# Selection of the samples' keys inside the prompt attention, a step for each head pair, on VectorE

## What is computed

```python
def indexer_select(q_idx, w_idx, k_idx, key_pos, q_pos, n_sel):
    r = jax.nn.relu(jnp.einsum('qhd,sd->qhs', q_idx, k_idx).astype(jnp.float32) * IDX_DIM ** -0.5)
    score = jnp.einsum('qh,qhs->qs', w_idx.astype(jnp.float32), r)
    causal = key_pos[None, :] <= q_pos[:, None]
    _, sel = lax.top_k(jnp.where(causal, score, -jnp.inf), n_sel)
    return sel, key_pos[sel] <= q_pos[:, None]

# a sample: 256 of its 8193 positions; then the rows of keys and values at these positions
        sel, valid = indexer_select(qi, wi, keys_idx, key_pos, q_pos, n_sel)
        k_sel = gather_rows(cache_k, pages, kd, sel, past)
        v_sel = gather_rows(cache_v, pages, vd, sel, past)
```

## Time and profile before

| | us |
|---|---|
| median of 3 runs | 3193.95 (3188.23 to 3194.69) |
| profiled execution | 3187.16 |
| its span, from the first to the last instruction | 3185.3 |
| PE busy in the span | 2648.2 (83%) |
| DVE busy | 1513.6 (48%) |
| ACT busy | 1101.4 (35%) |
| mean granted TensorE clock | 0.921 of full speed |

### The profile page before, as it was taken

How to read it: one execution, slowest core, us unless ns; L and a number is a source line. 1 busy time by engine, 2 the same in 40 slices (tenths; PEclk the granted TensorE clock), 3 DMA queues, 4 the chain that set the end, 5 groups by cost and what they waited for, 6 DMA issues and landing times. The chain is left out here.

```text
span 3185.3 us, 43012 instructions
## 1 busy us (share of the span) xinstructions
PE 2648.2 (83%) x14536; PEld 1497.1 (47%) x14536; DVE 1513.6 (48%) x3685; ACT 1101.4 (35%) x2366; POOL 339.7 (11%) x355
## 2 busy tenths in 40 slices
PE   4798995859988898959878449895989899999978
PEld 1344443538777787845555434343333333333323
DVE  0256454568778786846655755384111111111116
ACT  0223222559876796836444001121111111111111
POOL 0000001010010100011100022043000000100015
PEclk8899997979999999968999779998999999999989
DMA  9312125332171121133100054122999878887867
GB/s 380 137 57 85 47 57 184 126 109 68 37 273 56 67 67 51 34 119 76 31 16 8 8 200 146 69 78 89 392 342 344 342 277 312 321 316 256 303 229 308
DMA packets 242838, 510.69 MB, mean 160 GB/s; under 512 B 23029, under 2 KB 101055, under 8 KB 235248
## 3 DMA queue, kind: packets, MB, share of 16 engines
q1 hardware_dynamic: 195396, 328.71, 29.8%
q0 software_dynamic: 28352, 126.04, 10.8%
q10 hardware_dynamic: 18932, 53.91, 4.3%
HBM read 618.22 MB, written 87.01 MB: 221 GB/s over the span
## 5 line engine op out<-in xcount | busy, mean ns | idle before, releaser
L2740 PE MATMUL routed_ex_pG<-routed_ex_WG,routed_ex_XT 128*64 128x512 f32 x2048 | 485.9, 618 | 69.3 <-issue 29.9
L1838 DVE TENSOR_REDUCE ssqc<-SQ 128x8 f32<-128x512 f32 x516 | 346.2, 683 | 132.9 <-ACT SQ L1644 120.1
L1559 PE MATMUL eK<-WA,LT 128*128 128x272 f32 x1032 | 328.1, 400 | 0.0
L1556 PE MATMUL eK<-dWkv,LT 128*128 128x256 f32 x1032 | 318.3, 391 | 10.9 <-ACT SQ L1644 10.5
L2832 DVE COPY routed_ex_XT<-routed_ex_pX 128x512 f32<-128x512 f32 x128 | 85.6, 689 | 503.6 <-PE routed_ex_pX L2727 503.5
L1644 ACT ACTIVATE SQ<-eK 128x512 f32<-128x512 f32 x516 | 292.5, 603 | 57.0 <-PE eK L1559 41.3
L2740 PEld LDWEIGHTS routed_ex_pG<-routed_ex_WG,routed_ex_XT 128*64 128x64 f32 x2048 | 140.6, 141 | 326.3 <-issue 303.7
L536 PE MATMUL in_pp<-ada_Win,in_hT 128*128 128x512 f32 (+1 forms) x640 | 281.7, 599 | 9.8 <-ACT in_pr L450 9.8
L2760 PE MATMUL routed_ex_pY<-routed_ex_WD,routed_ex_AT 128*64 128x512 f32 x1024 | 232.4, 595 | 1.6 <-DMA routed_ex_WD<-in_w_e_down 1.6
L1559 PEld LDWEIGHTS eK<-WA,LT 128*128 128x128 f32 x1032 | 201.5, 195 | 29.2 <-DVE numc L1837 0.2
L1556 PEld LDWEIGHTS eK<-dWkv,LT 128*128 128x128 f32 x1032 | 191.2, 197 | 46.8 <-ACT SQ L1644 15.6
(11 more groups left out here) (532 smaller groups left out, 3774.2 us busy)
## 6 DMA issues: line engine op xcount, KB each, us to landing
routed_ex_WG<-in_w_e_gu SPq DMA_DIRECT2D x128, 2048.0 KB
routed_ex_WD<-in_w_e_down SPq DMA_DIRECT2D x128, 1024.0 KB
s_yblk<-routed_ex_Y ACTq DMA_DIRECT2D x64, 512.0 KB
ada_Wada<-in_w_ada SPq DMA_DIRECT2D x8, 3072.0 KB, 16.9
s_yblk<-zrows SPq DMA_DIRECT2D x15, 1024.0 KB, 13.7
ada_Win<-in_w_in ACTq DMA_DIRECT2D x4, 2048.0 KB, 18.5
s_tdT<-in_td SPq DMA_DIRECT2D x8, 832.0 KB
s_h<-out_h ACTq DMA_DIRECT2D x9, 512.0 KB, 2.6
```

Source lines behind the costliest of these rows:

```text
L1556: pe.matmul(pK[kn % 3][:, 512 + z:512 + z + HK], key, Wkv[:, 4:8, 0:NOPE], start=True, stop=True)
L1559: pe.matmul(pK[kn % 3][:, z:z + HK + 16], key, WA[:, pr, :], start=True, stop=True).then_inc(s_KN, 1)
L1838: dve.tensor_reduce(ssqc[cg % 2][:, n - 1 - tau, :], SQ[kn % 4].rearrange("p (h d) -> p h d", h=H), AX.X, ALU.add).then_inc(s_red, 1)
L2740: m = pe.matmul(pG[u][r, :], XT[u][:, k, r], WG[2 * u + v][:, k, :], start=(k == 0), stop=(k == KD - 1))
```

## The change

`stage_sample` and `sample_select` are gone. Their work is a list of steps in `attend`, hung on the item number n. On DVE a step is done behind the multiply of pair n-1 (and behind the prompt's own selection step, if there is one), and always before the maxima of pair n+2: `page_rows` at n = 1, `marks` at 2 to 5, `chosen` at 10 to 13, `numbered` at 16 to 19, `digits` at 20 to 22, and `place` at 24 to 55. `place` handles 16 slots (17 at the end of a pair) of one pair of samples: 32 chunks in place of four passes over 129 slots. On PE the products of a chunk stand ahead of the products with the values of the same item, in four column groups (partitions 0, 32, 64, 96 of `pO`); DVE reads their sums ahead of the multiply (`read_sums`) and adds them up in `zparts`. Totals follow at items 8 and 14, a fold over the four groups at item 58, the list's transpose at item 62. The list's transfers are issued by SP between the stores of tiles 6 and 7. `mb` has one buffer now, and POOL waits for the maxima of the tile before.

```diff
-        for st in (stage_ada, stage_in, stage_index, stage_prompt, stage_sample, stage_out, stage_dispatch, stage_routed,
+        for st in (stage_ada, stage_in, stage_index, stage_prompt, stage_out, stage_dispatch, stage_routed,
                    stage_combine):
...
-    mb = [sb(f"mb{i}", [P, H, 2 * P]) for i in range(2)]
+    mb = sb("mb", [P, H, 2 * P])
...
+    CHUNK0, TOTAL01, TOTAL2, FOLD, TURN = 24, 8, 14, 58, 62
+    chunks = [(pr, CH * x, CH * x + CH + (x == 7)) for pr in range(NP2) for x in range(8)]
...
             store(NT - 2)
+            sp.wait_ge(s_zw, 1)
+            for a, n in enumerate(("dpos", "drow")):
+                sp.dma_start(T[n].rearrange("n a b -> a n b"), zlst[:, :, 16 * a:16 * a + 16]).then_inc(s_zo, 16)
+            sp.wait_ge(s_zo, 32)
+            for a, n in enumerate(("dpos", "drow")):
+                sp.dma_start(zld[a], T[n].rearrange("n (s h a) b -> (n s h) (a b)", s=2, h=2)).then_inc(s_zi, 16)
             store(NT - 1)
...
-                if i >= 2:
-                    pool.wait_ge(s_nm, 16 * (i - 1))
+                if i >= 1:
+                    pool.wait_ge(s_nm, 16 * i)
...
                 if n >= 2:
                     pe.wait_ge(s_on, n - 1)
+                if n == TOTAL01:
+                    pe.wait_ge(s_zc, 1)
+                    pe.matmul(pO[0][:, 384:388], c("same_half"), zcnt[:, 0, :], start=True, stop=True)
+                    pe.matmul(pO[0][:, 388:392], c("before_half"), zcnt[:, 1, :], start=True, stop=True)
...
+                elif 0 <= n - CHUNK0 < len(chunks):
+                    k = n - CHUNK0
+                    pr, z, e = chunks[k]
+                    pe.wait_ge(s_zb, k + 1)
+                    for s in range(e - z):
+                        u = s % 4
+                        m = pe.matmul(pO[n % 2][32 * u:32 * u + 32, 256:288], zA[:, s, :],
+                                      zB[:, s, :, :].rearrange("p a b -> p (a b)"), start=(s < 4), stop=(s >= e - z - 4))
+                    m.then_inc(s_zm, 1)
+                elif n == FOLD:
+                    pe.wait_ge(s_zl, 1)
+                    pe.matmul(pO[0][0:32, 384:512], c("fold32"), zparts[:, :, :].rearrange("p n w -> p (n w)"), start=True, stop=True)
+                elif n == TURN:
+                    pe.wait_ge(s_zi, 32)
+                    for a in range(2):
+                        pe.transpose(pO[0][:, 384 + 16 * a:400 + 16 * a], zld[a], c("ident")[0:16, 0:16])
...
+            def place(k):
+                pr, a, b = chunks[k]
+                w = b - a
+                if k:
+                    dve.wait_ge(s_zm, k)
+                link(dve.tensor_tensor(zA[:, 0:w, :], zmark[:, pr, a:b].unsqueeze(2).to_broadcast([P, w, 32]),
+                                       c("iota")[:, 0:32].unsqueeze(1).to_broadcast([P, w, 32]), ALU.is_equal))
+                link(dve.tensor_tensor(zB[:, 0:w, 0, :], zrank[:, pr, a:b].unsqueeze(2).to_broadcast([P, w, 16]),
+                                       c("iota")[:, 0:16].unsqueeze(1).to_broadcast([P, w, 16]), ALU.is_equal))
+                link(dve.tensor_tensor(zB[:, 0:w, 1, :], zB[:, 0:w, 0, :], zrow[:, pr, a:b].unsqueeze(2).to_broadcast([P, w, 16]), ALU.mult))
+                dve.tensor_tensor(zB[:, 0:w, 0, :], zB[:, 0:w, 0, :], zpos[:, a:b].unsqueeze(2).to_broadcast([P, w, 16]), ALU.mult).then_inc(s_zb, 1)
...
             def norm(n):
                 i, g, p = items[n]
                 dve.wait_ge(s_O, n + 1)
+                read_sums(n)
...
                     if g == 1 and FIRST <= i + 1 < NT:
                         select(i + 1 - FIRST, p)
+                    if n == 1:
+                        page_rows()
+                    elif 2 <= n < 6:
+                        marks(n - 2)
+                    elif 10 <= n < 14:
+                        chosen(n - 10)
+                    elif 16 <= n < 20:
+                        numbered(n - 16)
+                    elif 20 <= n < 23:
+                        digits(n - 20)
+                    elif 0 <= n - CHUNK0 < len(chunks):
+                        place(n - CHUNK0)
```

More of the change, by code:

```diff
@@ L851, in attend @@
     more = sb("more", [P, NT - FIRST])
+    NP2, NSL, CH = NS // 2, PAGE + 1, 16
+    SD, sthr, gpos, grow = G["SD"], G["thr"], G["gpos"], G["grow"]
+    zmark, zrank, zrow = (sb(n, [P, NP2, NSL]) for n in ("zmark", "zrank", "zrow"))
+    zkey, zpos = sb("zkey", [P, NSL]), sb("zpos", [P, NSL])
+    zA, zB = sb("zA", [P, CH + 1, 32]), sb("zB", [P, CH + 1, 2, 16])
+    zcnt, zneed, zpg, zpo = sb("zcnt", [P, 3, NP2]), sb("zneed", [P, 2, NP2]), sb("zpg", [P, NP2]), sb("zpo", [P, 1])
+    zri = zA[:, :, :].rearrange("p a b -> p (a b)").bitcast(I32)[:, 0:NP2 * NSL].rearrange("p (n s) -> p n s", n=NP2)
+    zrj = zB[:, :, :, :].rearrange("p a b c -> p (a b c)").bitcast(I32)[:, 0:NP2 * NSL].rearrange("p (n s) -> p n s", n=NP2)
+    zparts = sb("zparts", [P, NP2, 32])
+    zlst = zB[0:32, 0:4, :, :].rearrange("p a b c -> p (a b c)").rearrange("p (n w) -> p n w", n=NP2)
+    zld = [zA[0:16, 4 * a:4 * a + 4, :].rearrange("p a b -> p (a b)") for a in range(2)]
+    zgr = sb("zgr", [P, 16])
+    s_zc, s_zb, s_zm, s_zl, s_zw, s_zo, s_zi = (sem("az_" + n) for n in ("count", "onehot", "placed", "parts", "list", "out", "in"))
+    CHUNK0, TOTAL01, TOTAL2, FOLD, TURN = 24, 8, 14, 58, 62
+    chunks = [(pr, CH * x, CH * x + CH + (x == 7)) for pr in range(NP2) for x in range(8)]
     pS = [[ps(f"aS{a}{b}") for b in range(2)] for a in range(2)]
@@ new lines, in chosen @@
+            def chosen(pr):
+                link(dve.scalar_tensor_tensor(out=zmark[:, pr, :], in0=zrank[:, pr, :], scalar=zneed[:, 0, pr:pr + 1], in1=zmark[:, pr, :],
+                                              op0=ALU.is_le, op1=ALU.mult))
+                link(dve.scalar_tensor_tensor(out=zmark[:, pr, :], in0=SD[:, pr, :], scalar=sthr[:, pr:pr + 1], in1=zmark[:, pr, :],
+                                              op0=ALU.is_gt, op1=ALU.add))
+                link(dve.tensor_tensor_scan(zrank[:, pr, :], ones[:, :].to_broadcast([P, NSL]), zmark[:, pr, :], 0.0, ALU.mult, ALU.add))
+                if pr == NP2 - 1:
+                    dve.tensor_copy(zcnt[:, 2, :], zrank[:, :, NSL - 1]).then_inc(s_zc, 1)
@@ new lines, in numbered, with digits @@
+            def numbered(pr):
+                link(dve.scalar_tensor_tensor(out=zrank[:, pr, :], in0=zrank[:, pr, :], scalar=zneed[:, 1, pr:pr + 1], in1=zmark[:, pr, :],
+                                              op0=ALU.add, op1=ALU.mult))
+                link(dve.tensor_scalar(zrow[:, pr, :], zkey[:, :], zpg[:, pr:pr + 1], None, ALU.add))
+            def digits(step):
+                if step == 0:
+                    link(dve.tensor_scalar(zri, zrank[:, :, :], -1024.0, None, ALU.add))
+                    link(dve.tensor_scalar(zrj, zri, 4, None, ALU.arith_shift_right))
+                elif step == 1:
+                    link(dve.tensor_copy(zmark[:, :, :], zrj))
+                    link(dve.tensor_scalar(zmark[:, :, :], zmark[:, :, :], c("half32"), None, ALU.add))
+                elif step == 2:
+                    link(dve.tensor_scalar(zrj, zri, 15, None, ALU.bitwise_and))
+                    link(dve.tensor_copy(zrank[:, :, :], zrj))
```

150 lines of the change are left out of this document (39 added, 111 removed).

## The result

| | before | after |
|---|---|---|
| median (20 runs each) | 3190.77 us | 3201.11 us |
| lowest to highest | 3186.08 to 3198.07 | 3193.91 to 3208.04 |
| profiled execution / its span | 3187.16 / 3185.3 | 3203.07 / 3201.3 |

The ratio is 1.0031, with an interval of 1.0024 to 1.0038: the change makes the kernel 0.3% **slower**. The forecast was 3172 with a range of 3150 to 3198, so both sign and range were wrong. The stage behind the attention did vanish as foreseen; the attention itself grew by more than the 87 us that this freed.

A forecast was written before the change was run, and what follows sets the result against it. No engine was full; from tile 4 a closed loop of DVE's maxima and copy and PE's sum rows, values and scores bound the attention. -87.0 + 30.2 + 8.7 + 9.4 + 6 + 14 = -18.7 us gave 3172, range 3150 to 3198.

The forecast's parts named there:

- gross gain: Between the starts of sample_select and the stage after it: 87.0 us, freed if that stage follows the attention directly.
- placement: DVE in rounds 24 to 55: 2.23 us each with its read, leaving 30.2 us in tiles 4 to 6 and 8.7 in tile 3.
- products: PE, between sum rows and values: 0.35 us per round, 8.4 us in tiles 4 to 6 and 1 in tile 3.
- clock: TensorE's granted clock falls after long PE waits, about 1.4 us each; entered as +14 us, 2 to 35.
- small steps: Rounds 1 to 22, 58 and 62: mostly covered by DVE's waits for values; 6 us, between 3 and 12.
- Costed at nothing: New chunk waits, POOL's wait with one masked bias, and SP's list transfers: none holds the work up, 0 us.
- The cover: DVE's waits for scores (18.1 us) and transposes (5.2) in tiles 4 to 6 absorb placement work and are all used up.
- the ring: From tile 4, a closed loop: DVE's maxima and copy, PE's sum rows and values, PE's scores; products on it count in full.
- column groups that don't overlap: Rival for PE's products: groups of 32 columns run one after another, 0.84 us more in 28 rounds, +24, 3196 us; chance 0.07.
- the floor: Rival for PE's products: matmul halves start at least 25 ns apart, 0.45 us more in 28 rounds, +13, 3185 us; chance 0.08.
- The rival in which it stays low over whole tiles: The clock doesn't come back between long waits, so tiles 4 to 6 run at 1.2 GHz: +43, 3215 us; chance 0.10.

The follow-up runs named there:

- the run with POOL's added wait: Changed kernel, but POOL's masked add for tiles 4 to 7 also waits until the same round's placement is done; 3182.69 us, ratio 0.9967 to the kernel before.
- the run with fillers: Changed kernel plus idle 96-column matmuls on PE ahead of its wait for DVE's copy, rounds 24 to 55; 3196.44 us, ratio 1.0015 to the kernel before.

## Why the prediction was wrong, point by point

With the attention's lengths from multiply to multiply (profiled executions, in us), the sum reads:

| term | forecast | measured |
|---|---|---|
| gross gain | -87.0 | -87.0 |
| rounds of tiles 3 to 6 (placement 38.9, products 9.4, clock 14) | 62.3 | 61.7 without the collision |
| collision of placement and POOL's add | 0 | 23.6 |
| small steps (tiles 1, 2 and 7) | 6 | 9.3 |
| later first multiply | 0 | 1.6 |
| sum | -18.7 | +9.2 |

The 61.7 is tiles 3 to 6 of the run with POOL's added wait less those of before (272.9 - 211.2); the 23.6 is how much longer they are in the changed kernel.

That 61.7 lies so near to 62.3 is in part luck. By the pieces measured below, the products of tiles 4 to 6 cost 24 x 0.54 = 13.0 for a forecast of 8.4, and without the collision the clock falls only 7 more times than before in tiles 3 to 6, some 10.5 us for the 14 entered.

- **The step that failed is the price of the placement**: "So 2.23 us in each of the 32 rounds 24 to 55." In four rounds the placement took 6.26 us and 0.22 for the read, 6.5 in all; the collision with POOL's add, which makes the difference, was put at nothing. The durations came from `sample_select`, where POOL had no instruction (1780 to 1856 us), and were taken to hold in the attention. "Costed at nothing" does speak of POOL: "One masked bias instead of two: POOL now also waits until the maxima of the tile before are done." That sentence holds, and the single `mb` isn't the cause, since POOL's adds of tiles 4 to 7 start at the selection's end in both kernels. But it asks only when POOL may start and who waits for it, not what runs on DVE while it adds. The placement is put directly behind the instruction that releases POOL, so the two meet at the end of each of the tiles 3 to 6. Nobody waits for the other by a semaphore, so a list of waits can't show it. None of the rivals names it either. With the 23.6 us taken off, the measured balance is -14.4 for a forecast of -18.7: right in sign and within 5 us.
- **It was to be read from the trace before.** In the routing stage, which I hadn't looked at, POOL works beside DVE as well (timeline, then min, median and maximum of two DVE lines in ns):

```profile
2144.81 2.46 POOL L2432 TENSOR_TENSOR dispatch_hY<-dispatch_hY,dispatch_hgf 128x1024 f32<-128x1024 f32 x1 [1.59 <-ACT dispatch_hY L2412]
2144.99 5.54 DVE L2634 TENSOR_SCALAR dispatch_gB<-K,dispatch_gblkf,dispatch_gtokf 128x80 f32<-128x80 f32 x6
```

```profile
L2634 DVE TENSOR_SCALAR dispatch_gB<-K,dispatch_gblkf,dispatch_gtokf x54: 305/310/2415, 2129.8 to 2164.1; 128x80 f32<-128x80 f32 x54
L2638 DVE TENSOR_TENSOR dispatch_gS<-dispatch_gS,dispatch_gGT x6: 757/758/2784, 2165.2 to 2180.7; 128x576 f32<-128x576 f32 x6
```

Here a median of 0.31 us has a maximum of 2.42, beside a POOL multiply of 2.46. L2634 reads one tensor in SBUF, as the copy above does. A maximum far from a median, in a group of one shape, is where to look.
- **The cover** was right. Every wait of DVE for scores in tiles 4 to 6 is gone, and away from the add the placement took 1.98 us and its read 0.22, together 2.20 for a forecast of 2.23. Where the clock stays up, the rounds come out as written: 42 and 43 at 7.77 and 44 at 9.88 in the run with fillers (forecast 7.7 and 9.7). In the changed kernel itself 44 took 11.29 with a fall (forecast 11), but 42 and 43 had a fall each as well and took 9.31 and 8.73.
- **The products** were mis-sized: 0.54 on the ring, for 0.35. The 16 products start 0.39 us ahead of the values, near the lower bound as chosen, but they bring 0.10 of a later start and 0.05 of longer values along. Of the rivals, column groups that don't overlap (1.19) are refuted. So is the floor: 32 halves in 0.39 us are 12 ns each. By the Trainium skill's rule of about 25 ns between starts (TensorE: Matmul & The Clock Gate, "Wait — 56ns, not 53.3ns?") they would have taken 0.8, an estimate from that page's figure. The measurement decides: in four column groups the starts lie closer together than that.
- **The clock** came out near its term in the changed kernel: 10 more stretches at 0.50 in tiles 3 to 6, at 1.5 us for each (from the nine rounds of the run with fillers), against 14 us in the sum. But three of the ten go with the collision, and those in its rounds are longer (6.8 to 10.2 us at 0.50, where most others last 3.4). The rival in which it stays low over whole tiles didn't come. PE in round 42 of the changed kernel, with the clock at 0.50 from 1655.95 to 1659.36 behind a wait of 1.79 us:

```profile
1655.73 0.52 PE L987 MATMUL aT<-K,rs 128*64 128x128 f32 x4 [1.79 <-DVE PT L1054]
1656.19 0.66 PE L1015 MATMUL aO<-zB,zA 128*32 128x32 f32 x32
1656.78 2.78 PE L1028 MATMUL aO<-PT,vmS 128*64 128x128 f32 x24
```

- **The small steps** were mis-sized, 9.3 for 6, within the 3 to 12 given. The falls of the clock that they bring were left out. In tile 1 the clock falls for 13.7 us (1464.8 to 1478.5) from round 13 on; tile 1 varies with it, 25.7 to 33.5 us in the profiled executions with the same steps. The steps can meet an add as well: in the run with POOL's added wait, `numbered` in round 16 has an instruction of 2.81 us (L1166, 0.34 in its other rounds) beside the add for tile 2, and the round takes 5.04 us instead of 3.66 in the changed kernel. In round 58 PE waits 1.39 us, does the fold, and runs the values at half clock, in 3.41 us instead of 1.92.
- **The other waits costed at nothing** did cost nothing: the single `mb` by the run without steps, and the list's transfers, which were issued by 1833.5, for a turn in pair 62.

With the four chunks moved and the products ahead of PE's wait the same idea gives 3148 us; as it was written it gives 3201.

## What to carry to other kernels

Before work is moved onto an engine, list what the neighbouring engines do in the same microseconds, and not only who waits for whom: here VectorE work on two SBUF tensors, and a plain SBUF copy, stood still beside a GpSimd add of 4.5 us until that add was done. Such work should not stand just behind the instruction that releases GpSimd; with GpSimd's start behind it the comparison was back at 0.44 us. And a row whose maximum is far from its median deserves a look in every stage, also those that the change does not touch.

## What the runs showed of the hardware that I had not expected

- A DVE copy of 64 elements in a row, SBUF to SBUF, took 4.39 us beside a POOL add of 4.51; a reduction of the same 64 took 0.22 beside the same add, and maxima with one operand in PSUM kept their 0.68.
- 32 matmul halves of 32 columns in four column groups took 0.39 us from their first start to that of the values behind them, 12 ns each; in one group they took 37 ns each.
- At the lower clock level the same 32 halves took 0.59 us to the start of the values (1656.19 to 1656.78 in the changed kernel), 1.5 times as much, while the 24 halves of values behind them took 2.78 instead of 1.48.
